# First norm by row blocks, a new order where the first feed forward opens, first tiles split by halves

## The chip, the cores and the metric

One core of a Trainium2 chip runs the whole program. The metric is the device time in microseconds (us) from one launch; the lower the better. Engines are named as in the profile: PE (TensorE, matrix products), PEld (its weight loads), DVE (VectorE), ACT (ScalarE), POOL (GpSimd), SP (the queue that issues most transfers).

## The reference, cut to what matters

Two transformer blocks run one after the other on x of 512 tokens by 1024, in float32.

```python
# first block
xn = rms_norm(x, norm1_w)
proj = xn @ w_in                    # q, k, v, hgrn parts, gates
x = x + mixed @ w_out               # mixed: sliding window attention and hgrn2
x = x + hierarchical_moe(rms_norm(x, norm2_w), ...)   # 32 experts, 2 per token
# second block
x = x + 0.5 * swiglu_ffn(rmsnorm(x, ffn1_norm), w_gate, w_up, w_down)   # ffn1
x = x + hybrid_mixer(rmsnorm(x, mix_norm), w_in, ...)                   # mixer 2
x = x + 0.5 * swiglu_ffn(rmsnorm(x, ffn2_norm), w_gate, w_up, w_down)   # ffn2
x = rmsnorm(x, final_norm)
```

## The kernel before, in words

**Products by halves of precision.** A dense product in float32 is done as three: every operand is cut into `hi` (rounded to what PE multiplies, by ACT, L1798) and `lo` (the remainder `raw - hi`, by DVE, L2198). A weight comes in units of at most 4 x 128 rows by 512 columns (1 MB); a unit has a `raw` buffer that SP's load fills, one of two `hi` and one of two `lo` buffers. `mm(key, ui, i, u)` multiplies unit number ui of a weight with row block i (128 tokens) of the activations: 4 x 3 = 12 products (L1499 to L1501, or L1503 to L1505), called a block here. Before its first product `mm` waits for the whole of `hi` (`a_hi`) and `lo` (`v_lo`) of its unit. In some places a unit is rounded in two halves, steps `("hi", u, 0)`, `("hi", u, 1)` and the same for `lo`; PE waits for the second half all the same.

**Norms.** For each of four row blocks tb: ACT squares and sums, DVE scales the sum, ACT takes the root, DVE inverts and writes `xs`, PE transposes `xs` into two PSUM banks (8 transposes), ACT copies them out as `xh` and DVE writes the remainder `xl`. The first norm, `n1`, does it otherwise: all four blocks are normed, 32 transposes (L1439) fill eight banks, each bank holding one 128-column piece for all tokens, and ACT (L1851) and DVE (L2314) multiply by the norm's weight while they copy out, bank by bank. The other norms (`ffn1`, `n2`, `ffn2`) multiply `xs` by a broadcast row of the weight (L2221) and go by row blocks (`turn_rows` and `turned`: L1449, L1819, L2229).

**Stages.** Mixer 1 begins with `n1` and the weights `qa` (units 0 and 1), `kv` (2 and 3), `qh` (4 and 5). Then come the experts, of whose last pair the results are written `back` by PE (L1416, L1417) and `added` to x by DVE (L2183); then ffn1, mixer 2 (`in2` weights after the norm `n2`; at its end `wo2(tb, c, half)`, PE L1733 to L1735), and ffn2 (row blocks in the order 3, 2, 1, 0).

**What sets the order.** The functions `schedule_*` write one list S of steps by hand; each engine runs its part of every step in the order of the list, and waits at semaphores. So a step that stands ahead of another on ACT, DVE or PE delays it there. A `hi` buffer is free again when the last product of the unit two before has read it; SP loads a `raw` buffer again when its `lo` is written. For the first two units of ffn2 both `hi` and `lo` wait for two `wo2` steps (`h4`), since the weights of `wo2` lie in these four buffers, and `turned` of ffn2 waits in ACT for the very last `wo2`.

```python
def norm_order(S, feed, name, order):
    for tb in order:
        S.append(("norm", name, tb))
    feed.split_to(feed.taken + 1)
    S.append(("turn", name))
```

## Time and profile before

| what | value |
|---|---|
| runs | 1828.27, 1830.04, 1830.62 us; median 1830.04 |
| profiled execution | 1829.55 us, of which the span 1827.7 |
| mean granted clock of PE | 0.987 |
| PE busy | 1755.2 us, 96% of the span |
| DVE, ACT, POOL busy | 920.1 (50%), 599.1 (33%), 12.5 us (1%) |
| chain that ended last | PE 86%, DMA 5%, DVE 4%, ACT 4% |
| transfers | 330.59 MB, mean 181 GB/s; about 420 GB/s from 460 to 900 us |

How to read it: the span is the profiled program on the chip, and the profiled execution's own time is 1.85 us more. PE is busy nearly throughout, so time is saved where it waits, or where its granted clock is half (its products then start 0.43 us apart where they else start 0.227 apart). Waits are read from the timeline: the number in brackets on a row is the idle time before it.

### The profile page before, as it was taken

Reading aid. Unit: us, or ns where it says so; the run is one execution under the profiler, and the core shown is the slowest. Engines: PE = TensorE matmul, PEld = TensorE weight load, DVE = VectorE, ACT = ScalarE, POOL = GpSimd, SP = SyncE. Lnnn points to the kernel's source line nnn. Section 1 sums busy time; section 2 is a strip of 40 time slices with the busy share of each in tenths; the row PEclk is TensorE's granted clock in tenths of the full one; section 3 lists DMA queues with packets and bytes.
Section 4 is the critical chain, followed back from the end, with each engine's and each line's share of the span. In section 5 each row is a group of like instructions: output and inputs, shape, how many; then the busy total and the mean of one; then the engine's idle time right before and its main releaser. Section 6 shows DMA issues by size and latency. Waiting matters only on the chain.

```text
span 1827.7 us, 19981 instructions
## 1 busy us (share of the span) xinstructions
PE 1755.2 (96%) x8340; PEld 1274.3 (70%) x8340; DVE 920.1 (50%) x1311; ACT 599.1 (33%) x900; POOL 12.5 (1%) x22
## 2 busy tenths in 40 slices
PE   7999999998999999999989999999999999999998
PEld 6777887785454445343478888887877778888886
DVE  4667864634232323232444845734577444745634
ACT  4456434442111111110143323323355333323322
...
GB/s 197 93 70 70 93 75 177 190 106 217 361 422 422 421 421 421 422 420 420 398 110 93 65 143 69 65 142 93 115 70 36 57 134 87 69 138 69 101 107 58
DMA packets 93167, 330.59 MB, mean 181 GB/s; under 512 B 6176, under 2 KB 15536, under 8 KB 68368
## 3 DMA queue, kind: packets, MB, share of 16 engines
...
q10 hardware_dynamic: 2304, 4.20, 0.6%
...
## 4 chain that ended last, share of the span: by engine, by line
PE 86%; DMA 5%; DVE 4%; ACT 4%; issue 1%; SPq 0%; DVEq 0%; ACTq 0%
PE PS L1503 11%; PE PS L1504 10%; PE PS L1505 10%; PE PS L1383 10%; PE PS L1499 5%; PE PS L1500 5%; PE PS L1501 5%; PE PS L1406 5%; PE PS L1478 3%; PE PS L1479 3%; PE PS L1477 3%; PE PS L1354 2%; DMA rawz<-in_w_up_experts 2%; PE PS L1355 2%; PE PS L1416 2%; PE PS L1576 2%
## 5 line engine op out<-in xcount | busy, mean ns | idle before, releaser
L2198 DVE TENSOR_TENSOR lo<-raw,hi 128x2048 fp32r<-128x2048 f32 (+2 forms) x142 | 254.2, 1794 | 317.8 <-ACT hi L1798 317.4
L1798 ACT CAST hi<-raw 128x1024 fp32r<-128x1024 f32 (+2 forms) x144 | 216.9, 1513 | 297.5 <-PE PS L1505 112.3
L1503 PE MATMUL PS<-xh_ffn,hi 128*128 128x512 f32 x576 | 225.0, 391 | 0.9 <-DVE SG L2409 0.9
L1505 PE MATMUL PS<-xh_ffn,lo 128*128 128x512 f32 x576 | 224.2, 389 | 0.0
L1504 PE MATMUL PS<-xl_ffn,hi 128*128 128x512 f32 x576 | 224.1, 389 | 0.0
L1383 PE MATMUL PS<-raw,XG 128*64 128x512 f32 x416 | 140.2, 601 | 5.0 <-DVE YL L2175 2.8
L1503 PEld LDWEIGHTS PS<-xh_ffn,hi 128*128 128x128 f32 x576 | 108.1, 188 | 23.6 <-issue 1.3
L1505 PEld LDWEIGHTS PS<-xh_ffn,lo 128*128 128x128 f32 x576 | 108.1, 188 | 22.5
L1504 PEld LDWEIGHTS PS<-xl_ffn,hi 128*128 128x128 f32 x576 | 108.2, 188 | 22.1
L2168 DVE TENSOR_TENSOR HF<-SG,PS 128x512 f32<-128x512 f32 x16 | 17.3, 1078 | 183.5 <-PE PS L1383 183.5
L1383 PE MATMUL PS<-rawz,XG 128*64 128x512 f32 x400 | 88.9, 593 | 2.9 <-DMA rawz<-in_w_up_experts 2.9
L2175 DVE SCALAR_TENSOR_TENSOR YL<-PS,SM,YH 128x512 fp32r<-128x512 f32 x32 | 22.5, 746 | 135.7 <-ACT YH L1781 135.7
L1383 PEld LDWEIGHTS PS<-raw,XG 128*64 128x64 f32 x416 | 43.3, 139 | 65.2 <-issue 61.6
L2183 DVE TENSOR_TENSOR x_sb<-x_sb,PS 128x512 f32<-128x512 f32 x128 | 78.3, 684 | 9.1 <-PE PS L1417 9.1
L1503 PE MATMUL PS<-xTh,hi 128*128 128x512 f32 x192 | 78.8, 411 | 2.1 <-DVE lo L2198 2.1
L1504 PE MATMUL PS<-xTl,hi 128*128 128x512 f32 x192 | 75.7, 394 | 0.0
L1505 PE MATMUL PS<-xTh,lo 128*128 128x512 f32 x192 | 75.6, 394 | 0.0
L1383 PEld LDWEIGHTS PS<-rawz,XG 128*64 128x64 f32 x400 | 29.4, 137 | 60.0 <-issue 59.8
L1773 ACT COPY HT<-PS 128x512 f32<-128x512 f32 x16 | 9.4, 587 | 182.6 <-PE PS L1392 182.6
L1406 PE MATMUL PS<-raw,HT 128*64 128x512 f32 x192 | 64.3, 595 | 1.3 <-ACT HT L1773 1.3
L1499 PE MATMUL PS<-hi,xh_ffn 128*128 128x512 f32 x128 | 51.1, 399 | 7.2 <-ACT xs_ffn L1802 3.1
L1781 ACT ACTIVATE YH<-PS,SM 128x512 fp32r<-128x512 f32 x32 | 20.3, 684 | 105.1 <-PE PS L1406 105.1
...
## 6 DMA issues: line engine op xcount, KB each, us to landing
raw<-in_w_in SPq DMA_DIRECT2D x26, 1024.0 KB, 5.1
raw<-in_w_gate_experts SPq DMA_DIRECT2D x26, 1024.0 KB, 15.6
raw<-in_w_up_experts SPq DMA_DIRECT2D x26, 1024.0 KB, 14.4
rawz<-in_w_up_experts SPq DMA_DIRECT2D x26, 1024.0 KB, 12.9
rawz<-in_w_down_experts SPq DMA_DIRECT2D x26, 1024.0 KB, 14.0
raw<-in_w_down_experts SPq DMA_DIRECT2D x24, 1024.0 KB, 13.3
rawz<-in_w_gate_experts SPq DMA_DIRECT2D x24, 1024.0 KB, 16.0
raw<-in_ffn_w_down SPq DMA_DIRECT2D x20, 1024.0 KB, 5.0
```

The lines of the kernel that those rows point to most:

```text
L1383: x = e.matmul(PS[64 * q:64 * q + 64, b, :], XG[(i // GP) % 2][:, k, s:s + 64], w[q][:, kk * 512:kk * 512 + 512], start=k == 0, stop=k == 7)
L1406: x = e.matmul(PS[64 * q:64 * q + 64, b + c, :], HT[:, j, 64 * q:64 * q + 64], w[q][:, jj * D + c * 512:jj * D + c * 512 + 512], start=j = ...
L1477: e.matmul(PS[:, b, :], xh[:, k, c], h[:, k, :], start=k == 0 and not g, stop=False, skip_group_check=g)
L1499: e.matmul(o, xh[:, k, c], h[:, kk, :], start=s0, stop=False)
L1500: e.matmul(o, xh[:, k, c], l[:, kk, :], start=False, stop=False)
L1501: x = e.matmul(o, xl[:, k, c], h[:, kk, :], start=False, stop=s1)
L1503: e.matmul(o, h[:, kk, c], xh[:, k, :], start=s0, stop=False)
L1504: e.matmul(o, h[:, kk, c], xl[:, k, :], start=False, stop=False)
L1505: x = e.matmul(o, l[:, kk, c], xh[:, k, :], start=False, stop=s1)
L1798: e.copy(q.hi[:, a:b], q.raw[:, a:b]).then_inc(*a_hi((u, 0) if part == 0 else u))
L2183: e.tensor_tensor(v, v, PS[:, b, :], ALU.add).then_inc(*m.v(("x", i, tb, c)))
L2198: e.tensor_tensor(q.lo[:, a:b], q.raw[:, a:b], q.hi[:, a:b].bitcast(F32), ALU.subtract).then_inc(*v_lo(key))
```

## The change: what it does

The first norm is done by row blocks, like the others: `first_rows` replaces `norm_order`. The norm's weight comes as a broadcast row (one more transfer of 512 KB), its multiplication moves into `xs` (an operation with three operands instead of two), and the copies out of PSUM lose it. The order of the first loads is new, a root of a dummy value is taken first on ACT (`warm_up`, a memset on DVE), unit 0 is rounded by halves, and the eight blocks of `qa` alternate between units 0 and 1. The two `kv` units are rounded before `rope` and `bounds` where one was before.

At the opening of ffn1 the results of the last experts go to fixed banks (`home`), the first weight tiles are rounded by halves, PE does unit 0 for row blocks 0 and 1 before unit 1, row blocks 2 and 3 are added and normed later, and the evictions of row blocks 0 and 1 stand together. At `n2` and ffn2 the first tiles are rounded by halves in a new order; ffn2's `hi` waits for the first two `wo2` steps of row block 0 and only its `lo` for the other two, and `turned` waits for the last `wo2` of its own row block. In `mm`, PE waits for the first half of a unit's `hi` and `lo`, and for the rest in the middle of the block, for each unit whose `lo` is made by halves (`halved`), in the old places too.

```diff
+def first_rows(S, feed):
+
+    def split(u):
+        S.extend([("hi", u), ("lo", u)])
+        feed.split += 1
+
+    S.append(("warm",))
+    S.append(("norm", "n1", 0))
+    S.extend([("hi", 0, 0), ("lo", 0, 0)])
+    S.extend(turn_steps("n1", 0, 4))
+    S.extend([("hi", 0, 1), ("lo", 0, 1)])
+    feed.split = 1
+    S.append(("norm", "n1", 1))
+    split(1)
+    n2, n3 = ("norm", "n1", 2), ("norm", "n1", 3)
+    staged(S, feed, ("qa",), [(0, 0), (1, 0), (0, 1), (1, 1), (0, 2), (1, 2), (0, 3), (1, 3)],
+           {(1, 0): turn_steps("n1", 1, 6) + [n2], (0, 1): [n3], (1, 1): turn_steps("n1", 2, 4), (0, 2): turn_steps("n1", 3, 6), (1, 2): [("split", 3)],
+            (0, 3): [("split", 4)]})
 
 
 def schedule_mixer1(S, p1):
 
     feed = Feed(S, p1, 0, 2)
     banks = Banks()
-    norm_order(S, feed, "n1", (0, 1, 2, 3))
-    dense(S, feed, ("qa",), 2, 4)
+    first_rows(S, feed)
...
+def schedule_opening(S, feed, tail):
+
+    n = tail.index(next(q for q in tail if q[:3] == ("combine", NP - 1, 0)))
+    home = {(0, 0): 4, (0, 1): 5, (1, 0): 0, (1, 1): 1, (2, 0): 6, (2, 1): 7, (3, 0): 2, (3, 1): 3}
+    u, key = feed.first, ("ffn1", "g", 0, 0)
+
+    def added(tb):
+        S.extend(("added", *q[1:4], home[q[2:4]]) for q in tail[n:] if q[2] == tb)
+
+    S.extend(tail[:n])
+    S.extend([("hi", u, 0), ("hi", u, 1)])
...
+    S.extend([("normed", "ffn1", 0), ("half", "ffn1", 1), ("rooted", "ffn1", 1), ("lo", u, 0)])
     S.extend(turn_steps("ffn1", 0, 4))
-    S.append(("mm", ("ffn1", "g", 0, 0), 0, 0, feed.first))
-    feed.split_to(2)
-    S.extend(norm_steps("ffn1", 1))
-    S.append(("mm", ("ffn1", "g", 0, 0), 1, 0, feed.first + 1))
-    S.append(("ev", ("ffn1", "g", 0, 0), 0))
-    S.extend(turn_steps("ffn1", 1, 6))
-
-
...
+    S.extend([("lo", u, 1), ("mm", key, 0, 0, u), ("scaled", "ffn1", 1), ("hi", u + 1, 0), ("hi", u + 1, 1), ("lo", u + 1, 0)])
+    S.extend(turn_steps("ffn1", 1, 4))
+    S.extend([("lo", u + 1, 1), ("mm", key, 0, 1, u)])
+    added(2)
+    S.extend(norm_steps("ffn1", 2))
+    added(3)
...
+        for ui, i in [(1, a), (1, b)] + rest:
+            if (ui, i) == (1, b):
+                S.extend(turn_steps(pre, c, 6) + norm_steps(pre, d))
             elif (ui, i) == (0, c):
-                S.extend(turn_steps(pre, d, 6))
+                S.extend([("ev", key, a), ("ev", key, b)] + turn_steps(pre, d, 4))
             elif (ui, i) == (1, c):
                 feed.split_to(3)
             S.append(("mm", key, ui, i, feed.first + ui))
-            if ui:
+            if ui and i in (c, d):
...
+        u = feed.first + feed.split
+        last[(1, 2)] = [("turn_rows", name, 1, 6), ("hi", u, 0), ("hi", u, 1), ("turned", name, 1, 6), ("lo", u, 0)]
+        last[(1, 3)] = [("lo", u, 1)]
+        feed.split += 2
     staged(S, feed, (pre, "d", p, 1), [(0, 0), (0, 1), (1, 0), (1, 1), (0, 2), (0, 3), (1, 2), (1, 3)], last)
-    S.append(("normed", name, 3))
+    if name == "final":
+        S.append(("normed", name, 3))
+    else:
+        S.extend([("hi", u + 1, 0), ("normed", name, 2), ("hi", u + 1, 1), ("normed", name, 3)])
...
-           {(0, 0): [("split", 2)], (0, 1): turn_steps("n2", 2, 4), (1, 0): turn_steps("n2", 3, 6), (0, 2): [("m2_bias",)],
+           {(1, 0): [("turn_rows", "n2", 2, 4), ("lo", u, 0), ("lo", u, 1), ("turned", "n2", 2, 4)], (1, 1): turn_steps("n2", 3, 6),
+            (0, 2): [("m2_bias",)],
...
-                    S.extend({(0, 0): [("turn_rows", "ffn2", 3, 4)], (0, 1): norm_steps("ffn2", 1), (1, 0): [("turn_rows", "ffn2", 2, 6)],
-                              (1, 1): [("half", "ffn2", 0)]}.get((c, half), []))
-                    if c and half:
-                        next_feed.split_to(1)
+                    u = next_feed.first
+                    S.extend({(0, 0): [("turn_rows", "ffn2", 3, 4)], (0, 1): norm_steps("ffn2", 1) + [("turned", "ffn2", 3, 4)],
+                              (1, 0): [("turn_rows", "ffn2", 2, 6), ("hi", u, 0), ("hi", u, 1)],
+                              (1, 1): [("lo", u, 0), ("lo", u, 1), ("turned", "ffn2", 2, 6), ("half", "ffn2", 0)]}[c, half])
...
-    S.extend([("turned", "ffn2", 3, 4), ("normed", "ffn2", 0), ("turned", "ffn2", 2, 6)])
-    next_feed.split_to(2)
+    u = next_feed.first + 1
+    S.extend([("hi", u, 0), ("hi", u, 1), ("lo", u, 0), ("normed", "ffn2", 0), ("lo", u, 1)])
+    next_feed.split = 2
...
-        place_ffn(first5, len(p5), l5, h4, [h4[0] + h4[2], h4[1] + h4[3]])
+        place_ffn(first5, len(p5), l5, h4, h4[0:2])
+        for j in range(2):
+            p5[j].lo_free = h4[2 + j]
...
+        halved = {q[1] for steps in (before, joint, after) for q in steps if q[0] == "lo" and q[2:] == (0,) and not U[q[1]].made}
...
+            load_x(0)
+            e.dma_start(rows["n1"][:, :], I["norm1_w"].partition_broadcast(128)[:, 0, :]).then_inc(*d_row["n1"](0))
+            e.dma_start(C1[:, 0:128], I["c_f32"][:, 0:128]).then_inc(*d_ident(0))
+            load(0, d_w)
+            load_x(1)
+            load(1, d_w)
+            for tb in range(2, NB):
+                load_x(tb)
+            e.dma_start(SM[:, 0:68], I["c_par"]).then_inc(*d_first(1))
+            load(2, d_w)
...
-                pe.wait_ge(a_hi, u)
-                pe.wait_ge(v_lo, u)
+                first = (u, 0) if u in halved else u
+                pe.wait_ge(a_hi, first)
+                pe.wait_ge(v_lo, first)
...
+                    if kk == q.kc // 2 and u in halved:
+                        pe.wait_ge(a_hi, u)
+                        pe.wait_ge(v_lo, u)
...
-                        act.wait_ge(p_m2, ("wo2", 0, 1, 1))
+                        act.wait_ge(p_m2, ("wo2", tb, 1, 1))
...
+            def warm_up():
+                act.wait_ge(v_norm, "warm")
+                e.activation(warm, warm, ACT.Sqrt).then_inc(*a_norm("warm"))
```

**Order at the start, DVE.** The rows in which DVE goes through the first norm and the `qa` weights (`lo_55`, `lo_56` are the two remainder buffers, `raw_49` to `raw_51` the loaded units); before:

```order
L2304 TENSOR_SCALAR SM<-SM 128x1
L2306 RECIPROCAL SM<-SM 128x1
L2308 TENSOR_SCALAR xs<-x_sb,SM 128x1024
L2198 TENSOR_TENSOR lo_55<-raw_49,hi_53 128x2048
L2314 SCALAR_TENSOR_TENSOR xTl<-PS,SM,xTh 128x512 x8
L2198 TENSOR_TENSOR lo_56<-raw_50,hi_54 128x2048
L2198 TENSOR_TENSOR lo_55<-raw_51,hi_53 128x1024
L2373 COPY qkn<-PS 128x512 x4
```

and in the change:

```order
L2330 SCALAR_TENSOR_TENSOR xs<-x_sb,SM,row_n_166 128x1024
L2212 TENSOR_TENSOR lo_55<-raw_49,hi_53 128x1024
L2250 TENSOR_TENSOR xTl<-PS,xTh 128x4x128 x2
L2212 TENSOR_TENSOR lo_55<-raw_49,hi_53 128x1024
L2325 TENSOR_SCALAR SM<-SM 128x1
L2327 RECIPROCAL SM<-SM 128x1
L2330 SCALAR_TENSOR_TENSOR xs<-x_sb,SM,row_n_166 128x1024
L2212 TENSOR_TENSOR lo_56<-raw_50,hi_54 128x2048
L2250 TENSOR_TENSOR xTl<-PS,xTh 128x4x128 x2
```

The first remainder and the first two copies now come before the second row block's norm, and the eight copies of L2314 are four pairs, spread among the products.

**Order at the opening of ffn1, DVE.** From the first norm's `xs` on; before:

```order
L2221 SCALAR_TENSOR_TENSOR xs_ffn_161<-x_sb,SM,row_ffn_166 128x1024
L2198 TENSOR_TENSOR lo_55<-raw_49,hi_53 128x2048
L2229 TENSOR_TENSOR xl_ffn<-PS,xh_ffn 128x4x128 x2
L2198 TENSOR_TENSOR lo_56<-raw_50,hi_54 128x2048
L2202 TENSOR_SCALAR SM<-SM 128x1
```

and in the change:

```order
L2225 RECIPROCAL SM<-SM 128x1
L2212 TENSOR_TENSOR lo_55<-raw_49,hi_53 128x1024
L2250 TENSOR_TENSOR xl_ffn<-PS,xh_ffn 128x4x128 x2
L2212 TENSOR_TENSOR lo_55<-raw_49,hi_53 128x1024
L2238 SCALAR_TENSOR_TENSOR xs_ffn_161<-x_sb,SM,row_ffn_167 128x1024
L2212 TENSOR_TENSOR lo_56<-raw_50,hi_54 128x1024
```

The remainders are cut in two and the second row block's `xs` stands between them (in this path the two `added` pairs of row blocks 2 and 3 follow later).

**Order at the opening of ffn2, ACT.** The rows from the norm of row block 2 (`xs_ffn_163`) on, `hi_53` and `hi_54` being the two rounding buffers; before:

```order
L1802 ACTIVATE xs_ffn_162,SM<-x_sb 128x512
L1798 CAST hi_53<-raw_49 128x2048
L1819 CAST xh_ffn<-PS 128x4x128 x2
L1808 ACTIVATE xs_ffn_162,SM<-x_sb 128x512
L1811 ACTIVATE SM<-SM 128x1
L1819 CAST xh_ffn<-PS 128x4x128 x2
L1798 CAST hi_54<-raw_50 128x2048
```

and in the change:

```order
L1834 CAST xh_ffn<-PS 128x4x128 x2
L1811 CAST hi_53<-raw_49 128x1024 x2
L1834 CAST xh_ffn<-PS 128x4x128 x2
L1815 ACTIVATE xs_ffn_162,SM<-x_sb 128x512
L1811 CAST hi_54<-raw_50 128x1024 x2
L1821 ACTIVATE xs_ffn_162,SM<-x_sb 128x512
```

The copies of the first row block and the first rounding are now ahead of the last norm's squares, where the wait for the last `wo2` had held them back.

## Rows read from the trace of the kernel before

**Rows 1.** The page, part 4: the chain that ended last, shares by engine.

```profile
PE 86%; DMA 5%; DVE 4%; ACT 4%; issue 1%; SPq 0%; DVEq 0%; ACTq 0%
```

**Rows 2.** PE timeline, first products after a wait (start us, us, engine line op; idle, releaser).

```profile
17.48 0.77 PE L1499 MATMUL PS<-hi,xTh 128*128 128x512 f32 x1 [2.36 <-ACT xTh L1851]
...
48.60 0.35 PE L1499 MATMUL PS<-hi,xTh 128*128 128x256 f32 x1 [1.87 <-DVE lo L2198]
...
67.54 0.47 PE L1503 MATMUL PS<-xTh,hi 128*128 128x512 f32 x1 [2.06 <-DVE lo L2198]
...
910.11 0.50 PE L1416 MATMUL PS<-YH,ST 128*128 128x512 f32 x1 [1.70 <-DVE YL L2175]
...
919.87 0.47 PE L1499 MATMUL PS<-hi,xh_ffn 128*128 128x512 f32 x1 [3.09 <-ACT xs_ffn L1802]
...
927.60 0.47 PE L1499 MATMUL PS<-hi,xh_ffn 128*128 128x512 f32 x1 [1.10 <-DVE xl_ffn L2229]
...
931.53 1.09 PE L1449 MATMUL PS<-C,xs_ffn 128*128 128x128 f32 x8 [0.94 <-DVE SM L2202]
...
1280.19 0.77 PE L1499 MATMUL PS<-hi,xh 128*128 128x512 f32 x1 [2.18 <-issue]
...
1464.87 0.76 PE L1499 MATMUL PS<-hi,xh_ffn 128*128 128x512 f32 x1 [2.98 <-ACT xs_ffn L1808]
```

**Rows 3.** Windows: busy us of PE, PEld, DVE, ACT, POOL; granted clock; DMA share; GB/s.

```profile
17.50:20.50 3.00, 3.00 (x7) 2.44 (x8) 3.00 (x6) 3.00 (x4) 0.00 (x0) 0.50 1.05 362
68.50:71.50 3.00, 3.00 (x8) 2.32 (x8) 2.93 (x7) 0.00 (x0) 0.00 (x0) 0.50 0.97 309
...
1280.00:1283.00 3.00, 2.81 (x7) 2.26 (x8) 1.91 (x5) 0.93 (x3) 0.00 (x0) 0.53 0.56 150
1465.00:1468.00 3.00, 3.00 (x8) 2.36 (x9) 2.70 (x6) 2.57 (x4) 0.00 (x0) 0.52 1.01 370
```

**Rows 4.** PE timeline in ffn2, the first products of two neighbouring blocks.

```profile
1476.38 0.39 PE L1499 MATMUL PS<-hi,xh_ffn 128*128 128x512 f32 x1
...
1479.10 0.39 PE L1499 MATMUL PS<-hi,xh_ffn 128*128 128x512 f32 x1
```

**Rows 5.** SP timeline of the x loads; DMA issues at 3.5 us (KB, us to landing).

```profile
1.66 1.85 SPq L1232 DMA_DIRECT2D x_sb<-in_x  x4
...
raw<-in_w_in SPq DMA_DIRECT2D x1, 1024.0 KB, 8.5
x_sb<-in_x SPq DMA_DIRECT2D x1, 512.0 KB, 6.3
```

**Rows 6.** ACT timeline, kv stage: a rounding of half size.

```profile
30.19 1.05 ACT L1798 CAST hi<-raw 128x1024 fp32r<-128x1024 f32 x1 [9.21 <-PE PS L1501]
```

**Rows 7.** DVE timeline: rope's first row, then the remainders that kv and qh wait for.

```profile
41.63 0.16 DVE L2319 CAST PF<-POS 128x4 f32<-128x4 int32 x1
...
47.24 1.22 DVE L2198 TENSOR_TENSOR lo<-raw,hi 128x1024 fp32r<-128x1024 f32 x1
...
66.18 1.22 DVE L2198 TENSOR_TENSOR lo<-raw,hi 128x1024 fp32r<-128x1024 f32 x1
```

**Rows 8.** Timeline, opening of the first feed forward: DVE, then ACT.

```profile
914.35 1.28 DVE L2221 SCALAR_TENSOR_TENSOR xs_ffn<-x_sb,SM,row_ffn 128x1024 f32<-128x1024 f32 x1
...
917.75 0.68 DVE L2229 TENSOR_TENSOR xl_ffn<-PS,xh_ffn 128x512 fp32r<-128x512 f32 x1
...
928.46 1.28 ACT L1811 ACT_TABLE_LOAD   x1
```

**Rows 9.** DVE timeline, the second mixer's first remainder.

```profile
1277.80 2.29 DVE L2198 TENSOR_TENSOR lo<-raw,hi 128x2048 fp32r<-128x2048 f32 x1 [1.01 <-ACT hi L1798]
```

**Rows 10.** Opening of the second feed forward: SP timeline, DMA issue, DVE timeline.

```profile
1452.88 0.37 SPq L1237 DMA_DIRECT2D raw<-in_ffn_w_gate  x1
...
raw<-in_ffn_w_gate SPq DMA_DIRECT2D x1, 1024.0 KB, 5.0
...
1461.24 2.29 DVE L2198 TENSOR_TENSOR lo<-raw,hi 128x2048 fp32r<-128x2048 f32 x1 [4.00 <-ACT hi L1798]
```

More of the change, by code:

```diff
@@ L866, in program @@
         ident, ones = cst("ident"), cst("ones")
-        n1c, n2c, f1c, mxc, f2c = (SM[:, 8 * i:8 * i + 8] for i in range(5))
+        n2c = SM[:, 8:16]
         psc = SM[:, 40:44]
@@ L967, in program @@
         xs_f2 = [at(f"xs{tb}_ffn2", o, [128, D]) for tb, o in enumerate((104, 88, 84, 80))]
-        rows = {n: at(f"row_{n}", o, [128, D]) for n, o in (("ffn1", 92), ("n2", 28), ("ffn2", 108))}
+        rows = {n: at(f"row_{n}", o, [128, D]) for n, o in (("n1", 88), ("ffn1", 92), ("n2", 28), ("ffn2", 108))}
         fxh, fxl = at("xh_ffn", 48, [128, 8, T], F32R), at("xl_ffn", 64, [128, 8, T], F32R)
@@ L1001, in program @@
         ot = at("ot", 32, [128, NB, D])
-        d_first, d_const, d_late, d_out = (sig("d_" + n, 16) for n in ("first", "const", "late", "out"))
+        d_ident, d_first, d_const, d_late, d_out = (sig("d_" + n, 16) for n in ("ident", "first", "const", "late", "out"))
         d_x = [sig(f"d_x{i}", 16) for i in range(NB)]
@@ L1008, in program @@
         d_zr = [sig(f"d_zr{i}", 16) for i in range(2)]
-        d_row = {n: sig("d_row_" + n, 16) for n in ("ffn1", "n2", "ffn2")}
+        d_row = {n: sig("d_row_" + n, 16) for n in ("n1", "ffn1", "n2", "ffn2")}
         d_r, d_b, d_bt = sig("d_router", 16), sig("d_small", 16), sig("d_bias", 16)
@@ L1137, in program @@
         schedule_moe(experts_again, True)
-        opening = []
-        feed3, feed5 = Feed(opening, p3, first3, 2), Feed(after, p5, first5, 2)
-        schedule_opening(opening, feed3)
+        joint = []
+        feed3, feed5 = Feed(joint, p3, first3, 2), Feed(after, p5, first5, 2)
+        n = next(j for j, q in enumerate(experts) if q[:3] == ("gu", "g", NP - 3))
+        experts, experts_tail = experts[:n], experts[n:]
+        experts_tail.insert(1 + next(j for j, q in enumerate(experts_tail) if q[:2] == ("turn_h", NP - 1)), ("table",))
+        n = schedule_opening(joint, feed3, experts_tail)
+        opening = [q for q in joint[n:] if q[0] not in ("back", "added")]
         feed3.steps = after
@@ L2054, in route @@
                 e.activation(e2, e2, ACT.Exp).then_inc(*a_rt("e2"))
[L2056 removed]
+            todo = {"warm": warm_up, "norm": norm, "turned": turned, "rope": rope, "bounds": bounds, "ev": ev, "at_square": at_square, "at_qT": at_qT,
                     "at_kT": at_kT, "at_scores": at_scores, "at_turn": at_turn, "at_values": at_values,
```

114 lines of the change are left out of this document (35 added, 79 removed).

## The prediction

> **What bounds the kernel now.** I read the chain of work that ended last first: PE has 86% of it [rows 1]. So the program takes as long as PE's own list, plus what PE waits, plus what it loses while its clock is granted at half. Then I went through PE's timeline for rows with idle time before them. Those in the places that the change touches are 2.36 us before the first product, 1.87 at `kv`, 2.06 at `qh`, then 3.09, 1.10 and 0.94 where ffn1 opens, 2.18 at the second mixer and 2.98 at ffn2 [rows 2]. The 1.70 at 910.11 waits for results of the experts, which nothing here brings sooner. Third, the windows: after four of these waits PE's granted clock is 0.50 to 0.53, the lower level of 1.2 GHz [rows 3]. Seven products then start in 3.00 us, 0.43 apart, where a block of twelve otherwise takes 1479.10 - 1476.38 = 2.72 us, 0.227 apart [rows 4]. Each such stretch covers about seven products, so it costs 7 x 0.2 = 1.4 to 1.5 us. After 1.87 us (48.60) and 3.09 us (919.87) the next rows show no slow products, so the length of the wait alone does not decide it.
>
> **The change, place by place.** PE's products are the same, so nothing else on its list counts.
>
> *Start.* Before, the fourth x block, issued at 1.66 + 1.85 - 0.44 = 3.07 us, lands 6.3 later at 9.4 [rows 5] with 2146 KB of transfers up to it; the first `qa` unit lands at 3.55 + 8.5 = 12.05. In the new order 2112 KB stand up to and with that unit, and the first x block, issued third at 1.66, is now first, two issues of 1.85 / 4 = 0.46 sooner: the unit lands between 8.5 and 9.4. I take 8.6, since the x block opens the queue. The norm of row block 0 is done by then (`xs` is 1.28 [rows 8]), whether or not its broadcast row is a bit slow. From there half a rounding, 1.05 [rows 6], half a remainder, 1.22 [rows 7], and the first copy, 0.68 [rows 8], with 0.1 for signals: first product at 11.6 instead of 17.48. But DVE is now the bound. It does the second copy, the second half (to 13.4), the small steps of row block 1 (0.65 with ACT's root), `xs` 1.28 (15.3), and after ACT's whole rounding the remainder of unit 1, 2.29 [rows 9]: 18.0. PE meanwhile does one block, at half clock, and 8 transposes, and waits. From 18.0 it has seven blocks, 19.0, and 16 transposes, 2 x 1.09 [rows 2]: `qa` ends at 39.2. Before, it ended at 17.48 + 8 x 2.72 + 1.5 = 40.8, with all transposes hidden. **Gain 1.6**; bounds 0 (another half-clock stretch after the wait for unit 1) and 2.5. So most of the six microseconds by which the first product comes sooner are not kept.
>
> *`kv`.* The wait of 1.87 is for a remainder that starts at 47.24, behind `rope` and `bounds` on DVE, which run from 41.63 [rows 7]. It is now ahead of them; it needs 1.05 + 1.22 after `qa`, and four short blocks cover that. What is late next is `qh`'s first remainder: `rope` now starts 3.1 us after `qa`'s end instead of 0.8, its 5.6 us, the rounding and 2.29 end 11.8 after it, where the two `kv` units end 11.7 after it. **Gain 1.7**, bounds 1.2 and 1.87.
>
> *`qh`.* The second unit is made by halves already; PE waits 2.06 for the half that begins at 66.18 and ends at 67.40 [rows 7], although it has the first half. Now it starts at 65.5, does six products (1.36) and waits some 0.5: 1.5 gained. The stretch at half clock from 68.5 to 71.5 [rows 3] follows on that wait; I count 0.9 of its 1.5, because the attention's first operands on DVE are ready about when PE would come for them. **Gain 2.4**, bounds 1.2 and 3.0. These three carry through mixer 1 and the experts, since SP issues every later load when a buffer comes free, not at a fixed time.
>
> *ffn1.* DVE is busy nearly throughout. From `xs` of row block 0 at 915.6 [rows 8] it now does: small steps, half a remainder, the copies (2 x 0.68), half a remainder, `xs` of block 1, half, copies, half, two additions, `xs` of block 2, two additions, copies, `xs` of block 3. Adding up, with about 0.08 of overlap at each, PE starts at 918.3 instead of 919.87, then waits 0.4 for the second half, 0.7 for copies, 0.3 and 1.2 for the last two `xs`: 4.2 us of waits instead of 3.09 + 1.10 + 0.94 = 5.13. One of the table loads (1.28, at 928.46 [rows 8]) stood in that path and goes. **Gain 0.9**, bounds 0 and 2.
>
> *n2.* The first product waited for a remainder of 2.29 that began at 1277.80 [rows 9]. A half of 1.22 begins at about the same time, behind the same copies: product at 1279.3 instead of 1280.19. Whether the half clock at 1280 [rows 3] goes too is open, since 1.5 us of wait remain; I leave it. **Gain 1.1**, bounds 0.7 and 2.5.
>
> *ffn2.* The load issued at 1452.88 lands 5.0 later, at 1457.9 [rows 10]. The rounding used to wait for the third `wo2` step, and DVE wrote the remainder from 1461.24 to 1463.53 [rows 10], then an addition and a copy. Now two half roundings end at 1460.0, the remainders at 1460.2 and 1461.4, and the copies of the first row block are done long before; `wo2` ends at 1461.8. PE goes on without a wait: 2.98 gained, and the half clock from 1465 [rows 3], 1.5, should go with it. **Gain 4.5**, bounds 3.0 (clock) and 4.6.
>
> **The sum** is 1.6 + 1.7 + 2.4 + 0.9 + 1.1 + 4.5 = 12.2. The profiled execution took 1829.55, its span 1827.7 and 1.85 around it, 0.49 below the median 1830.04; less 12.2 that is 1817.4 us. The lower bounds sum to 6.1, 1823.5; the upper ones to 15.8, 1813.7.
>
> The table load at 928.46 takes 1.28 [rows 8]; in the timeline ACT's work stands directly before and behind it, and the sum counts it at that. The Trainium skill (ScalarE: Activation LUTs, What ACT_TABLE_LOAD costs) gives the same 1283 ns for the load and adds about 1380 ns of drain to each switch. No such drain is in this trace; by the page ffn1 would gain some 1.4 more, 1816.0.
>
> **The rivals.**
> (1) *The clock falls anyway.* Waits of 1.5 us are left in three places, and shorter ones than those of now may be enough: 1.70 was, at 910.11. Then the 1.5 at ffn2 and the 0.9 at `qh` are not gained, and the start loses one more stretch: 12.2 - 1.5 - 0.9 - 1.5 = 8.3, 1821.2. Against it: at ffn2 nothing is left to wait for. The Trainium skill (TensorE: Matmul & The Clock Gate, Part 1) says that the number of slow products in a warm-up differs between runs of one kernel. By that rule the clock's terms could come out on either side, and the two waits above without slow products agree with it.
> (2) *Waits move to DVE.* It is the engine behind every term up to n2, and its own list grows by four three-operand `xs` and a dozen split remainders. If attention or the openings absorb what start, `qh` and ffn1 give, 1.7 + 1.1 + 4.5 = 7.3 is left: 1822.2. For it, `xs` of the first norm costs 1.28 where a two-operand one stood; against it, DVE is at 50% of the span, idle for PE several times between `qh` and the experts.
> (3) *Slower.* One mechanism: stopping and starting at the beginning, with transposes between the blocks, keeps the clock at half through `qa`. A block then takes 12 x 0.43 = 5.1 instead of 2.72, 2.4 more. The other terms give 10.6, so it decides from five further blocks on; with all eight the start loses 19.2 - 1.5 - 1.6 = 16.1 instead of gaining, the others' 10.6 leave 5.5 lost: 1835.0. Against it: the stretch after 17.48 was over after some seven products [rows 3], with the products back to back as they are again from the third block on.
> (4) *The change does little*: a forgotten wait keeps PE where it was at ffn2, and 7.7 is left: 1821.9.
>
> **How the numbers follow.** Forecast 0.70, rival 1 0.10, rival 2 0.10, rival 4 0.07, rival 3 0.03. The range goes from 1813.5, the upper bounds, to 1823.5, the lower bounds, which holds rivals 1, 2 and 4 as worked out. 0.2% of this kernel, 3.7 us, is about what a measurement can tell from none. Faster by more than that: 0.93; within it 0.04; slower 0.03.
>
> **What would show it.** In the new profile: first product at 11 to 12.5 us and `qa`'s last at 39 to 40; no wait at `kv` over 0.5; at `qh` a wait under 1 us in the middle of a block; 4 to 4.5 us of waits where ffn1 opens; about 1.5 at n2; none before ffn2's first product, with a clock of 1.00 there. Wrong would be a first product after 14 us, a half clock at ffn2, or new waits of over 1 us in attention.

## The result, and the profile after

| | before | after |
|---|---|---|
| median of the runs, us | 1830.33 (4 runs, 1828.27 to 1831.13) | 1816.38 (4 runs, 1815.84 to 1819.96) |
| ratio, 95% interval | | 0.9931 [0.992, 0.9943] |
| span of the profiled execution, us | 1827.7 | 1814.8 |
| mean granted clock | 0.987 | 0.991 |

The median is 14 us lower, and by the ratio, which is clear of 1, the changed kernel is 0.7% faster. The forecast was 1817.4. PE's share of the chain of work that ended last rose from 86% [rows 1] to 87%.

I compare by places. The same instruction is looked up in both traces, and the differences of its start give the gain of what lies between two such places:

| from, to (start in the trace before, after) | gain | forecast |
|---|---|---|
| start to the end of `qa` (40.82, 39.86) | 0.96 | 1.6 |
| to `qh`'s first block (54.42, 51.70) | 1.76 | 1.7 |
| to the transposes of `kd` (77.07, 71.06) | 3.3 | 2.4 |
| to the first product of the experts' last step (910.11, 905.10) | -1.0 | 0 |
| to the second norm's first `xs` (1270.54, 1264.38) | 1.15 | 0.9 |
| to the second softmax (1373.59, 1365.33) | 2.1 | 1.1 |
| to the wait for `SG` in ffn2 (1512.77, 1499.83) | 4.7 | 4.5 |
| sum (rest of the program: 0) | 12.9 | 12.2 |

The last line but one begins at the second softmax, so it holds the opening of ffn2.

PE's timeline after, the rows with idle time that answer to [rows 2] (start, busy, operation, then in brackets the idle time and what ended it):

```profile
12.77 0.77 PE L1512 MATMUL PS<-hi,xTh 128*128 128x512 f32 x1 [3.00 <-ACT hi L1811]
64.51 0.47 PE L1516 MATMUL PS<-xTh,hi 128*128 128x512 f32 x1 [0.29 <-DVE lo L2212]
146.04 1.97 PE L1561 MATMUL PS<-C,sA 128*128 128x128 f32 x8 [2.97 <-DVE sA L2522]
913.15 0.47 PE L1512 MATMUL PS<-hi,xh_ffn 128*128 128x512 f32 x1 [1.45 <-DVE xl_ffn L2250]
918.44 0.47 PE L1512 MATMUL PS<-hi,xh_ffn 128*128 128x512 f32 x1 [1.05 <-DVE xl_ffn L2250]
929.00 1.09 PE L1458 MATMUL PS<-C,xs_ffn 128*128 128x128 f32 x8 [1.16 <-DVE xs_ffn L2238]
1273.37 0.47 PE L1512 MATMUL PS<-hi,xh 128*128 128x512 f32 x1 [1.52 <-ACT hi L1811]
1275.14 0.47 PE L1512 MATMUL PS<-hi,xh 128*128 128x512 f32 x1 [0.17 <-DVE lo L2212]
```

The waits of 1.87 at `kv` and 2.98 at ffn2 are gone, 2.06 at `qh` has become 0.29, and where ffn1 opens 3.66 is left of 5.13. The window rows after (columns as in [rows 3]: granted clock third from the end):

```profile
12.00:15.00 3.00, 2.23 (x5) 1.82 (x6) 2.69 (x7) 2.28 (x5) 0.00 (x0) 1.00 1.04 403
64.50:67.50 3.00, 2.99 (x13) 2.50 (x14) 2.93 (x6) 1.32 (x2) 0.00 (x0) 1.00 0.59 175
147.00:150.00 3.00, 3.00 (x15) 1.85 (x14) 0.38 (x1) 1.53 (x3) 0.00 (x0) 0.65 0.70 268
1273.00:1276.00 3.00, 2.47 (x10) 1.80 (x11) 2.73 (x6) 1.02 (x4) 0.00 (x0) 1.00 0.00 0
1456.00:1459.00 3.00, 3.00 (x19) 2.56 (x18) 2.69 (x5) 1.48 (x5) 0.00 (x0) 1.00 1.03 397
```

The first of them reads 1.00 though its products are slow; the last section comes back to it. At `qh`, n2 and ffn2 the half clock of before is gone. At 147 there is one that before did not have: behind the wait for `sA`, which is as long as it was (2.98 at 152.07 then, 2.97 now), before had this row:

```profile
153.00:156.00 3.00, 3.00 (x18) 2.09 (x17) 0.41 (x1) 2.57 (x5) 0.00 (x0) 1.00 0.68 261
```

It costs 1.4 (169.05 us from `sA` to the products named `ho`, the transposes behind a wait of 2.92 in both kernels; before 167.64); 0.4 comes back on the way to the experts' last step, which leaves the -1.0 of the table.

At the start, from ACT's and DVE's timelines:

```profile
9.72 1.04 ACT L1811 CAST hi<-raw 128x1024 fp32r<-128x1024 f32 x1 [3.81 <-DMA raw<-in_w_in]
16.48 2.29 DVE L2212 TENSOR_TENSOR lo<-raw,hi 128x2048 fp32r<-128x2048 f32 x1 [0.31 <-ACT hi L1811]
```

The first tile landed at 9.72 (forecast 8.6), so the first product came at 12.77 (forecast 11.6) and the second block, behind the remainder that begins at 16.48, at 18.88 (forecast 18.0).

### The profile page after: what moved, and what is told of

It reads as the page before. It is cut to its first block, busy times and chain, and to the rows that moved or that the text cites. A ratio compares the mean times of both kernels' runs of the same rounds, so it can differ in the third digit from the quotient of the medians.

```text
span 1814.8 us, 20023 instructions
## 1 busy us (share of the span) xinstructions
PE 1751.4 (97%) x8340; PEld 1272.3 (70%) x8340; DVE 921.7 (51%) x1319; ACT 595.5 (33%) x905; POOL 12.5 (1%) x22
## 4 chain that ended last, share of the span: by engine, by line
PE 87%; DVE 5%; DMA 4%; ACT 4%; issue 1%; SPq 0%; DVEq 0%; ACTq 0%
PE PS L1516 10%; PE PS L1518 10%; PE PS L1517 10%; PE PS L1403 10%; PE PS L1512 5%; PE PS L1514 5%; PE PS L1513 5%; PE PS L1426 5%; PE PS L1488 3%; PE PS L1487 3%; PE PS L1486 3%; PE PS L1374 2%; PE PS L1375 2%; PE PS L1589 2%; DMA rawz<-in_w_up_experts 2%; PE PS L1436 2%
## 5 line engine op out<-in xcount | busy, mean ns | idle before, releaser
L2212 DVE TENSOR_TENSOR lo<-raw,hi 128x1024 fp32r<-128x1024 f32 (+2 forms) x149 | 255.1, 1717 | 321.3 <-ACT hi L1811 321.1
L1436 PE MATMUL PS<-YH,ST 128*128 128x512 f32 x128 | 52.9, 413 | 1.7 <-DVE YL L2187 1.7
## 6 DMA issues: line engine op xcount, KB each, us to landing
rawz<-in_w_up_experts SPq DMA_DIRECT2D x26, 1024.0 KB, 12.5
```

The lines of the kernel that those rows point to most:

```text
L1436: e.matmul(PS[:, b, :], ST[i % 2][:, tb, :], YH[:, c, :], start=True, stop=False)
L2212: e.tensor_tensor(q.lo[:, a:b], q.raw[:, a:b], q.hi[:, a:b].bitcast(F32), ALU.subtract).then_inc(*v_lo(key))
```

## The experiments

Spans are of the profiled execution, against 1814.8 of the changed kernel. One span says little, since stretches of half clock shift it: fourteen runs of the kernel before, taken together, go from 1827.8 to 1836.24 us. So here are the lengths of five stages for all kernels, read off as above: to `kd`; from there to the last expert step; ffn1 to the second norm; second mixer to its softmax; softmax to `SG` in ffn2. The rest, `SG` to the end, is 314.9 to 315.0 everywhere.

| kernel | start | experts | ffn1 | n2 | ffn2 | span |
|---|---|---|---|---|---|---|
| before | 77.07 | 833.04 | 360.43 | 103.05 | 139.18 | 1827.7 |
| after | 71.06 | 834.04 | 359.28 | 100.95 | 134.50 | 1814.8 |
| whole_tiles | 73.58 | 834.61 | 360.59 | 104.83 | 136.46 | 1825.0 |
| ffn2_old_frees | 70.74 | 833.76 | 359.32 | 100.91 | 141.33 | 1821.0 |
| ffn2_old_copy | 70.99 | 832.26 | 359.43 | 100.87 | 141.08 | 1819.6 |
| ffn2_frees_only | 70.80 | 834.87 | 359.31 | 100.96 | 134.58 | 1815.5 |
| kv_old_order | 74.60 | 835.32 | 359.61 | 100.93 | 136.07 | 1821.5 |
| load0_halves | 70.12 | 832.56 | 359.28 | 100.93 | 134.50 | 1812.3 |
| unit1_halves | 70.83 | 832.80 | 360.63 | 100.95 | 136.08 | 1816.2 |
| n2_rest_first | 70.89 | 834.66 | 359.37 | 99.80 | 134.52 | 1814.2 |
| kept_busy | 71.04 | 832.01 | 359.33 | 100.90 | 134.54 | 1812.8 |
| before_busy | 78.68 | 832.63 | 362.90 | 103.06 | 139.27 | 1831.5 |
| all_and_busy | 69.50 | 833.44 | 359.70 | 99.81 | 134.52 | 1811.9 |

Where a kernel's code does nothing new its stages mostly agree within 0.4 us. There are two exceptions, which count below: the experts' stage spreads over 3.1 us in kernels that are the same there (ffn2_old_copy 832.26, kv_old_order 835.32), and single stages come out 1.3 to 2.5 longer, where a stretch of half clock has appeared or fallen on other products.

**1. PE waits for whole tiles: whole_tiles.** The first tiles are still rounded by halves, in the new order; PE alone no longer begins with the first half.

```diff
-        halved = {q[1] for steps in (before, joint, after) for q in steps if q[0] == "lo" and q[2:] == (0,) and not U[q[1]].made}
+        halved = set()
```

> The change, with PE again waiting for a unit's whole hi and lo everywhere. Waits theory: at qh the wait of 0.29 grows to about 2 us (1.5 to 1.8 lost), and half clock behind it costs 1.4 more; the start loses 0.8, the second mixer's first block 1.2, ffn1's opening 0.2, ffn2 nothing: 5 us slower than the change, 3.7 without the clock. Rival (the new orders alone made the gain, half waits are worth nothing): 0 to 1 us slower.

Measured, 10 runs: 1826.54 us (1820.86 to 1827.48), ratio to before 0.9973 [0.9963, 0.9983]; span 10.2 longer than the change, where 5 were expected. PE's timeline:

```profile
14.21 0.77 PE L1512 MATMUL PS<-hi,xTh 128*128 128x512 f32 x1 [4.42 <-DVE SM L2325]
65.65 0.47 PE L1516 MATMUL PS<-xTh,hi 128*128 128x512 f32 x1 [1.65 <-DVE lo L2212]
917.93 0.47 PE L1512 MATMUL PS<-hi,xh_ffn 128*128 128x512 f32 x1 [3.13 <-DVE lo L2212]
1279.50 0.77 PE L1512 MATMUL PS<-hi,xh 128*128 128x512 f32 x1 [3.25 <-issue]
```

and its windows:

```profile
1279.00:1282.00 3.00, 2.50 (x6) 2.05 (x7) 2.62 (x6) 1.79 (x5) 0.00 (x0) 0.50 0.47 109
1374.00:1377.00 3.00, 3.00 (x10) 1.57 (x7) 1.40 (x2) 0.00 (x0) 0.00 (x0) 0.50 0.38 78
```

By stages it loses 2.5 at the start (the wait at `qh` alone grows by 1.65 - 0.29 = 1.36), 1.3 at ffn1, 3.9 at n2, and 2.0 at ffn2. The experts' stage has the other 0.6. At n2 some 2.6 of the 3.9 is thirteen products at half clock from 1279.50 on, 0.43 apart. In ffn2's stage the loss is a half clock behind the softmax's wait (1374), where this experiment changes nothing; **ffn2's opening has no wait here either: beginning with a half tile is worth at most 0.4 there** (2.0 less the 1.6 of that half clock).

Beside the kernel before, this run shows what the new orders do without the half tiles. `kv` begins at 40.99 (before 40.82), the ffn1 stage takes 360.59 (360.43) and n2 104.83 (103.05), of which 2.6 is half clock (1.5). **So at the start of `qa`, at ffn1 and at n2 the gain hangs on PE beginning with half a tile**; `kv` (11.85 us from its start to `qh`, as in the change, before 13.60) and ffn2 gain by the order, and `qh` has 0.4 less to wait and no half clock behind it. The size is less sure than the direction: three of the ten runs took 1820.9 to 1822.4 us at a mean clock of 0.991 or 0.992, and seven, the profiled one among them, 1825.1 to 1827.5 at 0.987 or 0.988. Against the change's median the loss is 4.5 to 6 us in the first group, near the 5 expected, and 9 to 11 in the second. What rounding in two pieces is worth by itself this leaves untried.

**2 to 4. The opening of ffn2 taken apart.** ffn2_old_copy lets the copies of the turned rows wait for the last product of the mixer again; ffn2_old_frees undoes that and the rule that frees the remainders' buffers apart from the others; ffn2_frees_only undoes the rule alone.

```diff
-                        act.wait_ge(p_m2, ("wo2", tb, 1, 1))
+                        act.wait_ge(p_m2, ("wo2", 0, 1, 1))
...
-        place_ffn(first5, len(p5), l5, h4, h4[0:2])
-        for j in range(2):
-            p5[j].lo_free = h4[2 + j]
+        place_ffn(first5, len(p5), l5, h4, [h4[0] + h4[2], h4[1] + h4[3]])
```

> The change, with only ffn2's turned waiting for the very last wo2. If ACT's queue is what counts (the copy holds back the roundings behind it), the first product waits 3.3 us, as much as with both undone or more, 4.5 to 4.8 slower. If the earlier release of hi is what counts, it waits 0 to 1 us.

> The change, with ffn2's first hi waiting for two wo2 steps again and turned waiting for the very last one. Waits theory: ffn2's first product waits about 3 us again, and a stretch at half clock follows: 4.5 us slower than the change. Rival (the clock there is chance): 3.0. Rival (the order alone did it): 0.

> Of the change at the opening of the second feed forward only the rule for the buffers is undone (both rounded parts of the first tile wait until hi and lo buffers of the tile before are free); the copy of the turned rows keeps its new, earlier release. With both undone the loss was 6.8 us between 1365 and 1500, with the copy alone 6.6. Theory A (each of the two is needed, so the losses do not add): hi starts only at about 1453.5, when the last product of the mixer has read the buffers, instead of 1450.21; PE waits 2 to 3 us for it and loses 3 to 5 us with a half-clock stretch behind the wait. Rival B (the copy is all there is to it, the buffers count for nothing): no wait, within 0.5 us of the changed kernel.

Measured: ffn2_old_copy 1821.65 us, one run; ffn2_old_frees, 5 runs, 1823.0 us (1822.07 to 1824.39), ratio to before 0.9958 [0.9939, 0.9977]; ffn2_frees_only 1817.49 us, one run. ffn2_old_copy in the timelines of ACT and PE:

```profile
1451.95 1.07 ACT L1834 CAST xh_ffn<-PS 128x512 fp32r<-128x512 f32 x2 [10.86 <-PE PS L1748]
1452.91 2.00 ACT L1811 CAST hi<-raw 128x1024 fp32r<-128x1024 f32 x2
1455.69 0.77 PE L1512 MATMUL PS<-hi,xh_ffn 128*128 128x512 f32 x1 [3.83 <-DVE lo L2212]
```

two windows of it:

```profile
1456.00:1459.00 3.00, 3.00 (x8) 2.33 (x8) 3.00 (x6) 2.78 (x5) 0.00 (x0) 0.50 0.44 103
1459.00:1462.00 3.00, 3.00 (x15) 2.42 (x14) 2.70 (x5) 0.92 (x4) 0.00 (x0) 0.66 0.75 286
```

and ACT's timeline in the changed kernel, then in ffn2_frees_only:

```profile
1450.21 2.00 ACT L1811 CAST hi<-raw 128x1024 fp32r<-128x1024 f32 x2 [6.40 <-DMA raw<-in_ffn_w_gate]
```

```profile
1451.64 2.00 ACT L1809 CAST hi<-raw 128x1024 fp32r<-128x1024 f32 x2 [7.20 <-PE PS L1746]
```

The held copy stands at the head of ACT's queue for 10.86 us, and the roundings behind it cannot start though their tile has landed: PE waits 3.83. Behind the wait it loses about 2.8 more in a half-clock stretch, 6.6 together, and 6.8 with both undone, where 4.5 to 4.8 were expected; the kernel before was 4.7 behind the change here. The buffers' rule costs 0.2 with the copy held and 0.1 without (the rounding starts at 1451.64 in a kernel that stood 0.6 later already, so 0.8 late, and still in time). My theory A for ffn2_frees_only fell: **the gain at ffn2 hangs on the earlier release of one copy.** In the old order the first rounding stood ahead of this copy on ACT; in the new one both halves stand behind it, and a held copy holds them too, which is why undoing this one line costs more (6.6) than the whole change of this place gained (4.7). That the early release is needed in the new order is shown. What it would give in the old order no run tried, so how the 4.7 divides between release and order is not shown.

**5. The remainder for `kv` behind `rope` again: kv_old_order.**

```diff
-           {(1, 0): turn_steps("n1", 1, 6) + [n2], (0, 1): [n3], (1, 1): turn_steps("n1", 2, 4), (0, 2): turn_steps("n1", 3, 6), (1, 2): [("split", 3)],
-            (0, 3): [("split", 4)]})
+           {(1, 0): turn_steps("n1", 1, 6) + [n2], (0, 1): [n3], (1, 1): turn_steps("n1", 2, 4), (0, 2): turn_steps("n1", 3, 6), (1, 2): [("split", 3)]})
```

> The change, with the second kv unit rounded behind rope and bounds again. Waits theory: a wait of 1.8 to 1.9 us is back in the middle of kv, and qh's first product comes 1.7 later, the rest unchanged behind it. Rival (DVE is late anyway and sets qh's start): the wait is back but qh starts within 0.5 us of the change's 51.70.

Measured: 1823.28 us, one run. The wait is back in PE's timeline:

```profile
47.66 0.55 PE L1511 MATMUL PS<-hi,xTh 128*128 128x256 f32 x1 [2.00 <-DVE lo L2211]
```

and behind it a half clock in the windows:

```profile
48.00:51.00 3.00, 3.00 (x16) 3.00 (x16) 2.29 (x1) 0.41 (x2) 0.00 (x0) 0.51 0.76 214
```

The start loses 3.5: 2.00 for the wait, and 1.5 for a clock that such a wait in the kernel before did not cost (1.87 at 48.60 in [rows 2], 1.00 in the window from 48 to 51). The wait was forecast, the clock was not: `qh`'s first product comes 3.2 later instead of 1.7. The span's other 3.2 lie in stages whose code is unchanged: 1.3 at the experts, 0.3 at ffn1, and 1.6 at the softmax.

**6. What the spread row costs: row_not_broadcast.**

```diff
-e.dma_start(rows["n1"][:, :], I["norm1_w"].partition_broadcast(128)[:, 0, :]).then_inc(*d_row["n1"](0))
+e.dma_start(rows["n1"][:, :], I["x"][0, 384:512, :]).then_inc(*d_row["n1"](0))
```

> Left out: the norm's weight row comes from rows of x instead of being spread over 128 partitions from one row, so the norm of the first mixer is scaled by other numbers. In the changed kernel the first weight tile landed at 9.72 us, where I had forecast 8.6. Theory A (the spread row, which now goes ahead of it, takes more of the DMA engines' time than its bytes say): the tile lands by 8.9 to 9.0, the first product starts at about 12.0 instead of 12.77, and the end comes 0.7 us earlier. Rival B (the queue alone, any transfer ahead of it costs the same): landing stays at 9.7 and nothing moves.

This kernel leaves the norm's weight out and loads ordinary rows of x in its place, as many bytes.

ACT's and PE's timelines:

```profile
8.95 1.04 ACT L1811 CAST hi<-raw 128x1024 fp32r<-128x1024 f32 x1 [2.99 <-DMA raw<-in_w_in]
12.00 0.76 PE L1512 MATMUL PS<-hi,xTh 128*128 128x512 f32 x1 [2.50 <-ACT hi L1811]
```

The tile lands 0.77 sooner and the first product comes 0.77 sooner, near the 0.7 to 0.8 of theory A. The list of DMA issues (size, median us from issue to landing), in the changed kernel and here:

```profile
row_n<-in_norm_w SPq DMA_DIRECT2D x1, 512.0 KB, 5.2
```

```profile
row_n<-in_x SPq DMA_DIRECT2D x1, 512.0 KB, 4.4
```

The whole time, 2328.58 us, tells nothing: the first norm is scaled by other numbers, so tokens go to other experts, and more expert steps run (the last begins at 1399.21 here, at 905.10 in the change). What the 0.77 is worth at the end is therefore not shown.

**7 to 9. Three places where the change left a wait.** load0_halves loads the first tile in two transfers:

```diff
-            load(0, d_w)
...
+            e.dma_start(dst[:, 0:2, :], q.src[:, 0:2, :]).then_inc(*d_half(0))
+            e.dma_start(dst[:, 2:4, :], q.src[:, 2:4, :]).then_inc(*d_w[q.slot](0))
...
-                    act.wait_ge(d_w[q.slot], u)
+                    if u == 0 and part == 0:
+                        act.wait_ge(d_half, 0)
+                    else:
+                        act.wait_ge(d_w[q.slot], u)
```

unit1_halves rounds the second tile by halves:

```diff
-    split(1)
+    S.extend([("hi", 1, 0), ("hi", 1, 1), ("lo", 1, 0), ("lo", 1, 1)])
+    feed.split = 2
```

n2_rest_first puts both remainders ahead of the copies at the second mixer:

```diff
-        last[(1, 2)] = [("turn_rows", name, 1, 6), ("hi", u, 0), ("hi", u, 1), ("turned", name, 1, 6), ("lo", u, 0)]
-        last[(1, 3)] = [("lo", u, 1)]
+        last[(1, 2)] = [("turn_rows", name, 1, 6), ("hi", u, 0), ("lo", u, 0), ("hi", u, 1), ("lo", u, 1), ("turned", name, 1, 6)]
+        last[(1, 3)] = []
```

> The first weight tile is loaded by two transfers with a signal each, so the first half can be rounded when half of it has landed. Theory: the first half lands 1.3 to 1.5 us before 9.72, the first rounding starts as much earlier, the first product at 11.4 to 11.9 instead of 12.77; what follows then waits for the second half and the second tile, so of it 0.3 to 0.8 us stays at the end of the first projection (39.86 in the changed kernel). Rival: both halves share the same DMA engines with all that is in flight and land together near 9.7; nothing moves.

> The second tile of the first projection is rounded by halves too, as the first one is. Theory: the second block, which waits 0.77 behind the remainder of the whole tile (16.48 to 18.77), starts at 18.1 instead of 18.88, and 0.7 to 0.8 us of it stays at 70.3 instead of 71.06. Rival: more and shorter operations in front of the second norm delay the second turned row block by as much, and nothing is gained.

> At the opening of the second mixer both halves of the first tile are rounded before the copies of the second turned row block, where the changed kernel rounds the remainders after them and PE waits 1.52 for hi and 0.17 for lo (1273.37, 1275.14). Theory: both waits go, 1.7 us less at the start of the second softmax (1365.33), if nothing else stands in front. Rival: the copies of the turned rows, now later, are what PE waits for, and 0.5 or less is left.

Measured, one run each: 1814.14, 1818.04 and 1815.96 us. ACT's and PE's timelines of load0_halves, then PE's of n2_rest_first:

```profile
8.20 1.04 ACT L1818 CAST hi<-raw 128x1024 fp32r<-128x1024 f32 x1 [2.14 <-DMA raw<-in_w_in]
11.25 0.77 PE L1516 MATMUL PS<-hi,xTh 128*128 128x512 f32 x1 [1.54 <-DVE xTl L2257]
16.51 1.18 PE L1462 MATMUL PS<-C,xs 128*128 128x128 f32 x8
17.92 0.47 PE L1516 MATMUL PS<-hi,xTh 128*128 128x512 f32 x1 [0.23 <-issue]
```

```profile
1280.08 0.47 PE L1512 MATMUL PS<-hi,xh 128*128 128x512 f32 x1 [1.39 <-DVE lo L2212]
```

load0_halves: the first half lands 1.52 sooner and so does the first product, and 0.94 of it stays at `kd`, a little over the 0.3 to 0.8 expected. The first block ends only 0.56 sooner (16.51 against 17.07), since it now runs wholly at 0.43 per product.

unit1_halves gives nothing of its own (70.83, with a first product that was 0.22 sooner anyway). That is the rival's number, but not its reason. PE's timeline there:

```profile
17.80 1.11 PE L1459 MATMUL PS<-C,xs 128*128 128x128 f32 x8
18.67 0.48 PE L1513 MATMUL PS<-hi,xTh 128*128 128x512 f32 x1
```

The second block comes at 18.67 instead of 18.88, and PE waits for nothing from its first product on. DVE has the turned rows' `xs` no later than in the change (begun at 14.66 against 14.89), and the remainders are done at 18.2. But here, as in load0_halves, the whole first block runs 0.43 apart, 5.25 us from 12.55 to 17.80, where the change takes 4.30. What the finer rounding would give with as short a stretch as in the change is not shown.

n2_rest_first: both waits go, and one of 1.39 stands two blocks later in place of 0.30; 1.15 of 1.7 is kept, between the two theories.

unit1_halves is slower in ffn1 and at the softmax by 1.35 and 1.6, in code that it does not touch. For ffn1 the windows tell why, unit1_halves first, then the change:

```profile
912.00:915.00 3.00, 3.00 (x9) 2.38 (x8) 3.00 (x4) 0.76 (x1) 0.00 (x0) 0.54 0.49 107
907.00:910.00 3.00, 3.00 (x8) 2.33 (x8) 2.56 (x7) 2.18 (x8) 0.00 (x0) 0.50 0.35 133
```

In the change, as in the kernel before, the half clock behind the wait of 1.70 for the last experts' results falls on their products, ahead of a norm that PE waits for anyway. In unit1_halves it comes some 5 us later and falls on the first products of ffn1. ffn2_old_frees has it in neither place and needs 359.32 for ffn1 against 359.28 in the change: **a half clock ahead of a wait that another engine ends costs nothing here**.

**10 and 11. Filling the waits: kept_busy and before_busy.**

```diff
+            def busy(b, n):
+                taken(b)
+                for _ in range(n):
+                    e.matmul(PS[:, b, 0:512], ident, C1[:, 0:512], start=True, stop=True)
...
+                if (it, kb) == (7, 0):
+                    busy(b, 3)
                 pe.wait_ge(v_at, ("w", it))
```

with the same ahead of `ho` (3) and the routing (5); before_busy adds three ahead of the first product of ffn2 in the kernel before, and there each block waits for its bank (`taken`) ahead of its weights instead of behind them.

> The changed kernel with eleven products added that nobody reads: three ahead of the wait at 143 to 146, three ahead of the wait at 312 to 315, five ahead of the wait at 411 to 416. Nothing is removed and no wait is shorter. Theory A (the granted clock falls behind idle time of TensorE): no half clock at 146 to 149, at 411 to 422 it goes too, at 315 to 323 it is shorter or gone (a second wait of 2.25 stays there); 1.4 + 1 to 1.6 + 1.9 us less, so 3 to 5 us faster by the span. Rival B (the clock falls whatever TensorE does in the wait): the span stays within 1 us, or grows by what the added products cost.

> The kernel before, with three products that nobody reads added in the wait of 2.98 us at the opening of the second feed forward (1461.9 to 1464.9). Theory: the wait for the copy stays where it ended (about 2.98 less the added 2.6), and the half clock of the stretch behind it (0.52 at 1465 to 1468) is gone, so 1.4 to 1.6 us less between 1373.59 and 1512.77 (139.2 before). Rival: the half clock comes all the same, and nothing is gained.

Measured, one run each: 1814.57 and 1833.3 us. kept_busy in PE's timeline:

```profile
142.89 2.73 PE L1454 MATMUL PS<-C 128*128 128x512 f32 x6
146.02 0.66 PE L1568 MATMUL PS<-C,sA 128*128 128x128 f32 x4 [0.40 <-DVE sA L2532]
```

and in windows:

```profile
147.00:150.00 3.00, 3.00 (x18) 2.12 (x17) 0.36 (x1) 2.57 (x5) 0.00 (x0) 1.00 0.69 264
318.00:321.00 3.00, 3.00 (x9) 2.37 (x8) 0.21 (x1) 2.98 (x4) 1.50 (x2) 0.52 0.29 51
```

before_busy, the same two views:

```profile
1467.02 2.73 PE L1490 MATMUL PS<-C 128*128 128x512 f32 x6
1470.16 0.47 PE L1502 MATMUL PS<-hi,xh_ffn 128*128 128x512 f32 x1 [0.40 <-DVE xl_ffn L2232]
```

and

```profile
48.00:51.00 3.00, 2.29 (x14) 2.33 (x15) 2.50 (x2) 1.04 (x2) 0.00 (x0) 0.75 0.38 79
1377.00:1380.00 3.00, 2.73 (x8) 1.27 (x8) 1.27 (x2) 0.12 (x1) 0.00 (x0) 0.55 0.13 23
1469.00:1472.00 3.00, 2.60 (x10) 1.57 (x9) 2.70 (x6) 2.01 (x6) 0.00 (x0) 1.00 1.02 363
```

Behind two of the filled waits PE runs at full clock: at 147, and at 1469 in before_busy, where [rows 3] has 0.52. That is theory A for these two places. From `kd` to `ho` kept_busy needs 242.62 against 244.03 in the changed kernel, 1.4 less, and all_and_busy 242.67. But unit1_halves, which fills nothing, happened to have no half clock at 147 either, and needs 242.65. So it is the 1.4 us that is shown, and that filling is what took it away rests on two kernels with full clock against one of ten without filling that share the new start. At 318, behind a second wait of 2.25 that I had not filled, and behind the routing a half clock is still there; 2.0 of the 3 to 5 expected was measured, and 0.6 of it, which lies in the rest of the experts' stage, is within that stage's spread. before_busy gained nothing over its whole ffn2 stage, because the softmax ahead of it drew a half clock (1377) that the kernel before had not; and by 1377 it was 3.7 us later, through stretches of half clock, in code that up to there differs from that kernel only in the order of two waits ahead of a block.

**12. All together: all_and_busy** (experiments 7, 8, 9 and 10 in one kernel).

> The changed kernel with the load of the first tile in two transfers, the second tile rounded by halves, both halves of the second mixer's first tile rounded first, and the eleven added products. One by one the first, third and fourth gave spans of 1812.3, 1814.2 and 1812.8 against 1814.8; taken at the places where each works: 0.9, 1.15 and 2.0 us, and 0.5 for the second by its theory. If they add: a span of 1810.3, a time of 1811.9 and a ratio of 0.990 to before. Rival: stretches of half clock move to places that had none, as at 146 in the changed kernel, and give back up to 1.7 each: 1812 to 1815 us.

Measured, 5 runs: 1813.46 us (1811.18 to 1814.05), ratio to before 0.9898 [0.9882, 0.9914], beside 0.9931 [0.992, 0.9943] for the change. Each ratio is against its own runs of before, and the two intervals do not touch, so it is faster than both, by 1.0% of the kernel before and some 0.3% of the change. The stages at which it works add up (start 1.56, n2 1.14, and 1.4 between `kd` and `ho`, 4.1); the span is 2.9 shorter, and the missing 1.2 are in the experts (0.8) and ffn1 (0.4), which the spread of these stages covers. The median lies in the rival's 1812 to 1815, and the ratio is the theory's 0.990; of the rival's reason, half clock in places that had none, nothing shows at 147.

## Why the prediction was right, point by point

- **ffn2, 4.5 forecast, 4.7 measured.** The amount is right; of its reason only a part is. I had counted the halved roundings, the buffers and the copy together. Experiments 1 to 4 show that the new order stands or falls with the copy's release: 6.6 with it undone, 0.1 to 0.2 for the buffers, at most 0.4 for PE's start on a half tile.
- **`qh`, 2.4 and 3.3.** The wait went from 2.06 to 0.29, 0.2 better than the 0.5 that I wrote. The rest is the clock: I counted 0.9 of its 1.5, and all of it went.
- **`kv`, 1.7 and 1.76.** The wait is gone and nothing stands in its place, as worked out. kv_old_order brings 2.00 back.
- **Start, 1.6 and 0.96.** The term was mis-sized at its first step, the landing at 8.6. It was 9.72, and 0.77 of the 1.1 is what the row spread over the partitions costs more than ordinary rows ahead of the tile; I had priced every transfer ahead of the tile by its bytes. Everything behind shifted with it, up to the second block's 18.88. The step after that held: DVE, with the remainder of the second tile, bounds the second block, and of 4.7 us at the first product 0.96 are left at the end of `qa`. In unit1_halves PE has no wait there, and the second block still starts at 18.67 instead of 18.88, since the first one runs wholly at half clock; how much the bound itself is worth stays open. The first product, 12.77, lies outside the 11 to 12.5 that I had named as a sign.
- **ffn1, 0.9 and 1.15.** 3.66 us of waits where I had added up 4.2, so 1.5 less than before, of which 1.15 is left. Two table loads went and not one: before has them at 923.01, 928.46 and 933.32, the change only at 927.44. The drain of about 1380 ns that the Trainium skill (ScalarE: Activation LUTs, What ACT_TABLE_LOAD costs) adds to a table switch is not in the trace of before, where ACT's next row starts at 929.75, 0.01 behind the end of the load; with it the forecast here would have been 2.3.
- **n2, 1.1 and 2.1.** Here the amount of the wait was wrong and the clock made up for it. From the norm's `xs` to the first product it takes 8.99 us instead of 9.65, 0.66 less, and the middle of the block waits 0.17 again; I had 1.1. The half remainder did not begin at the same time: DVE's row

```profile
1272.05 1.22 DVE L2212 TENSOR_TENSOR lo<-raw,hi 128x1024 fp32r<-128x1024 f32 x1
```

  is 7.67 behind `xs`, where the whole one began 7.26 behind it, since the copies ahead of it had waited for ACT's two roundings. The other 1.5 is the half clock, which I had left open and priced at nothing.
- **Not forecast:** the half clock at 147, 1.4 lost. Rival 1 had such a loss, in other places. None of the three signs of being wrong came. No rival as a whole came true: the clock rose at ffn2, waits did not move to DVE (the largest new one is 1.45), and from 18.88 on `qa` ran at full clock.

So the sum, 12.2 against 12.9, is closer than its parts, and that is luck. Two terms of clock that I had halved or left out (0.6 and 1.5) stand against one that I did not see (1.4), a start that was 0.6 short and a wait at n2 that was 0.5 to 0.6 short. The upper bounds were added up wrongly: 2.5 + 1.87 + 3.0 + 2 + 2.5 + 4.6 is 16.5, not 15.8, so the range should have begun at 1813.1. The measured median, 1816.38, lies inside either way. What the Trainium skill (TensorE: Matmul & The Clock Gate, Part 1) says of slow products, that their number differs between runs, holds here well beyond a warm-up.
